# A four-layer transformer block in one launch: another order for the opening, for the modulation sums of one output phase, and for the store of the result

## The chip, the cores and the metric

The kernel runs on one core of one Trainium2 chip. The metric is the device time of one launch in microseconds (us). The time of the kernel before is the median of three runs.

## What is computed

One sequence of 512 tokens by 1024 features (`x`) goes through four layers; from the third on, 256 context tokens come beside it. Each layer first makes six modulation vectors from a condition vector `c`. The first layer, which the change is about, cut to what matters:

```python
cs = jax.nn.silu(c)
ada = cs @ w_ada[i] + b_ada[i]
sh1, sc1, g1, sh2, sc2, g2 = split(ada, 6)
u = x * (1.0 + sc1) + sh1
proj = u @ w_in
qk, v, o, gates = split(proj)
qk = silu(causal_dwconv(qk, conv_w, conv_b))
ig = gates[..., :H]
lf = log_sigmoid(gates[..., H:])
h = chunked_scan(q, k, v, cumsum(lf), ig)
y = (rms_heads(h, norm_g) * sigmoid(o)) @ w_out
x = layer_norm(ALPHA * x + (1.0 + g1) * y, ln_g, ln_b)
```

All of it is float32. What else follows is an FFN with a convolution, a second layer with differential attention, and two more layers with RMS norms, a Fourier mixer, neighbourhood attention and MLPs.

## The kernel before

The activations stand transposed in SBUF: `XT` is 8 tiles (`KT`) of 128 features by 512 tokens. Weights are consumed as a stream of **jobs**: job j is one block of 128 output features, 8 x 128 x 128 weights, 512 KB in `wst`. SyncE loads it into one of two places of `RAW` (`load_raw`, which waits on `lo_done`). A float32 product is made from high and low parts: ScalarE rounds `RAW` to `WH` (`round_hi` and `round_next`, four places), GpSimd subtracts to get `WL` (`lo`), and TensorE multiplies WH by the high part of the activation (`U1h`), WH by the low part (`U1l`), and WL by the high part. So a job is 8 tiles x 3 = 24 matmuls of 128x512 (`stream`). Semaphores `hi_done`, `lo_done`, `pe_job` and `bank_read` count jobs through rounding, low part, matmuls and evacuation. The work is a list of phases (`plan`): "qk" has jobs 0 to 15, "v" 16 to 23, "gate_o" 24 to 31, "res" 32 to 39 (the output projection of layer 0 with residual and LayerNorm statistics), then "up" from job 40 on. Each engine walks the same list with its own code, in the order in which the code is written.

Modulation vectors are **ada sums**: one `tensor_tensor_reduce` of 128x1024 on VectorE for each tile of 128 outputs (`ada_sum`, `ada_job`), with its input tile (512 KB) loaded by SyncE just behind a weight job (`load_ada`, which waits on `ada_done`). `ada_out` adds the bias for four of them into `MOD` and raises `ada_evac`.

The **opening** of the kernel before, engine by engine:

- SyncE loads the condition vector `CB`, then 16 ada tiles into the 8 places of `ADA0`, with the parameters `PRM`, the gate weights `GW`, the whole of `XT` (2 MB, one transfer, behind the 8th ada tile) and the weights of jobs 0 and 1 in between.
- VectorE makes the 16 ada sums, shifts first, scales next (L1650), then `G2` and `B2` for all tiles at once (L1699, L1700), and only then the low parts `U1l` tile by tile (L1688).
- ScalarE rounds `GW` and jobs 0 and 1, then makes `U1h` (L876) and `UF` (L877) of each tile.
- GpSimd makes `GWl` and the low parts of the weights (L556).
- TensorE runs the 24 gate matmuls first (L1421), then the jobs (L1513).
- VectorE then works out the gate rows (`GR`, `GM`, L1706 to L1719, with Exp and Ln on ScalarE, L882 and L883) before it reads the first job's bank with the convolution (`conv`, L1724 and L1726). At the head of the v phase TensorE waits for `gate_rows` and transposes them.

In the **res phase** VectorE's body does, for each job, first `ada_job` and then `epilogue`:

```python
for u in range(4):
    if brings_ada(p, i):
        ada_job(i - p["groups"][0], p["ada"], u)
    epilogue(i, p, u)
```

The epilogue waits for ScalarE's scaled copy `TT` of the bank, adds it to `XT` (L1773), shifts it (L1745) and sums (L1751, L1765). ScalarE squares the shifted tile (L936) before it rounds the next job. After the last job `ln` raises `z_sum`, on which TensorE waits to make the token sums (L1532).

At the **end** SyncE waits for all 8 tiles of `x_final`, stores the 2 MB of `XT` in one transfer (L516) and waits for it.

## Time and profile before

| | |
|---|---|
| median of 3 runs | 2910.82 us (2907.27 to 2913.71) |
| the profiled execution | 2915.03 us |
| its span, first to last instruction | 2913.2 us |
| TensorE busy | 2771.7 us, 95% of the span |
| VectorE / ScalarE / GpSimd busy | 1588.5 / 1047.9 / 1096.3 us |
| mean granted TensorE clock | 0.979 |
| loaded / stored | 322.67 MB / 2.10 MB |

The span is what the rows below are measured in; the profiled execution is 1.8 us longer than its span, and 4.2 us above the median. TensorE is the busiest engine by far, so the time is its busy time and the stretches in which it has nothing to do.

### The profile page before, as it was taken

The page shows a single profiled execution, that of the slowest core. Times are in us where ns is not written, and L with a number is a line of the kernel's source. Part 1 is how long each engine was busy: PE and PEld are TensorE (multiplying, and loading weights), DVE is VectorE, ACT ScalarE, POOL GpSimd, SP SyncE. Part 2 cuts the span into 40 slices and gives each one's busy share as a digit, 9 for nine tenths or more (in the row PEclk, how much of TensorE's full clock was granted, in tenths as well). Part 3 has the DMA queues.
Part 4 walks back from the last instruction along what each step waited for, and adds up shares of the span by engine and source line. Part 5 has one row for each costly group of instructions (what it writes and reads, how often), then busy time and mean ns, then how long its engine had stood idle before and what let it go on. Part 6 is the DMA issues. An engine that isn't in the chain of part 4 may idle for free.

```text
span 2913.2 us, 37874 instructions
## 1 busy us (share of the span) xinstructions
PE 2771.7 (95%) x13936; PEld 2382.2 (82%) x13936; DVE 1588.5 (55%) x2359; ACT 1047.9 (36%) x1695; POOL 1096.3 (38%) x510
## 2 busy tenths in 40 slices
PE   4998899999899899999899999999998999999998
PEld 3885788887776678877899999999997977778887
DVE  6536866966555669987622423755552486332111
ACT  3333353424366453424322322222223348433222
POOL 2440254445422254445422433323335233334442
PEclk9999899999999899999899999999999999999999
DMA  5351345553422135554111122333332122122322
GB/s 213 114 184 49 109 137 190 196 191 117 139 91 62 51 123 188 195 179 148 53 58 59 44 87 87 130 130 130 116 130 73 58 83 77 58 80 94 101 94 87
DMA packets 89816, 328.06 MB, mean 113 GB/s; under 512 B 9940, under 2 KB 10708, under 8 KB 89304
## 3 DMA queue, kind: packets, MB, share of 16 engines
q1 hardware_dynamic: 85392, 312.21, 31.7%
q10 hardware_dynamic: 4296, 14.17, 1.5%
q8 instruction: 78, 1.28, 0.2%
q14 instruction: 50, 0.41, 0.0%
HBM read 322.67 MB, written 2.10 MB: 111 GB/s over the span
## 4 chain that ended last, share of the span: by engine, by line
PE 57%; DVE 2%; POOL 1%; issue 1%; ACT 1%; DVEq 0%; ACTq 0%; POOLq 0%
PE pair L1511 26%; PE pair L1513 18%; PE bank L1513 4%; PE pair L1351 1%; PE pair L1367 1%; PE bank L1384 1%; PE bank L1351 1%; PE pair L1465 1%; PE bank L1441 0%; PE pair L1324 0%; PE bank L1324 0%; PE bank L1304 0%; PE bank L1293 0%; POOL UF L538 0%; DVE UF L2056 0%
## 5 line engine op out<-in xcount | busy, mean ns | idle before, releaser
L556 POOL TENSOR_TENSOR WL<-RAW,WH 128x1024 fp32r<-128x1024 f32 x392 | 986.6, 2518 | 1655.5 <-ACT WH L863 942.3
L863 ACT ACTIVATE WH<-RAW 128x1024 fp32r<-128x1024 f32 x260 | 273.4, 1051 | 328.7 <-PE pair L1511 161.6
L1650 DVE CUSTOM_DVE_ANT_0 ADA<-ADA,CB 128x1024 f32<-128x1024 f32 x128 | 231.9, 1817 | 116.3 <-DMA ADA<-in_ast 104.7
L1783 DVE SCALAR_TENSOR_TENSOR XT<-pair,GATE,XT 128x512 f32 (+1 forms) x96 | 72.0, 750 | 353.7 <-PE pair L1513 179.8
L1511 PE MATMUL pair<-Uh,WH 128*128 128x384 f32 x832 | 215.2, 339 | 3.1 <-issue 1.6
L1511 PE MATMUL pair<-Ul,WH 128*128 128x384 f32 x832 | 211.1, 334 | 0.0
L1511 PE MATMUL pair<-Uh,WL 128*128 128x384 f32 x832 | 211.0, 334 | 0.0
L1513 PE MATMUL bank<-U1h,WH 128*128 128x512 f32 x480 | 187.2, 390 | 0.0
L1513 PE MATMUL bank<-U1h,WL 128*128 128x512 f32 x480 | 186.8, 389 | 0.0
L1513 PE MATMUL bank<-U1l,WH 128*128 128x512 f32 x480 | 186.8, 389 | 0.0
L1513 PE MATMUL pair<-U1h,WH 128*128 128x512 f32 x448 | 175.5, 392 | 2.7 <-POOL WL L556 2.7
L794 ACT ACTIVATE WH<-RAW 128x1024 fp32r<-128x1024 f32 x132 | 139.0, 1054 | 106.3 <-DMA RAW<-in_wst 51.7
L1513 PE MATMUL pair<-Hh,WH 128*128 128x512 f32 x432 | 169.3, 392 | 8.2 <-DVE Hl L648 8.2
L1513 PE MATMUL pair<-U1l,WH 128*128 128x512 f32 x448 | 174.9, 390 | 0.0
L1513 PE MATMUL pair<-U1h,WL 128*128 128x512 f32 x448 | 174.9, 390 | 0.0
L1513 PE MATMUL pair<-Hl,WH 128*128 128x512 f32 x432 | 168.2, 389 | 0.0
L1513 PE MATMUL pair<-Hh,WL 128*128 128x512 f32 x432 | 168.1, 389 | 0.0
L1511 PEld LDWEIGHTS pair<-Uh,WH 128*128 128x128 f32 x832 | 150.1, 188 | 7.3 <-issue 5.3
L1839 DVE SCALAR_TENSOR_TENSOR TT<-pair,TT 128x512 f32<-128x512 f32 x64 | 44.3, 692 | 196.2 <-ACT TT L986 103.7
L1511 PEld LDWEIGHTS pair<-Ul,WH 128*128 128x128 f32 x832 | 150.2, 188 | 0.0
L1511 PEld LDWEIGHTS pair<-Uh,WL 128*128 128x128 f32 x832 | 150.2, 188 | 0.0
L1511 PE MATMUL pair<-Hh,WL 128*128 128x384 f32 x512 | 129.9, 334 | 0.0
(416 smaller groups left out, 6139.1 us busy)
## 6 DMA issues: line engine op xcount, KB each, us to landing
RAW<-in_wst SPq DMA_DIRECT2D x392, 512.0 KB, 3.5
ADA<-in_ast SPq DMA_DIRECT2D x192, 512.0 KB, 4.3
NB<-in_nbias ACTq DMA_DIRECT2D x8, 768.0 KB, 4.5
XT<-in_xt SPq DMA_DIRECT2D x1, 2048.0 KB, 15.4
STRIP<-in_strip ACTq DMA_DIRECT2D x8, 256.0 KB, 2.7
CB<-in_cb ACTq DMA_DIRECT2D x4, 512.0 KB, 4.0
out_xt<-XT SPq DMA_DIRECT2D x1, 2048.0 KB, 6.2
VN<-VN ACTq DMA_DIRECT2D x4, 384.0 KB, 4.5
```

What stands on the lines that cost most here:

```text
L556: pool.tensor_tensor(WL[:, s4], RAW[:, s2], WH[:, s4].bitcast(F32), ALU.subtract)\
L794: act.activation(WH[:, u], RAW[:, u % 2], ACT.Copy).then_inc(S("hi_done"), 1)
L863: act.activation(WH[:, c % 4], RAW[:, c % 2], ACT.Copy).then_inc(S("hi_done"), 1)
L1351: mm = pe.matmul(BANK[b][:], x[:, k, tok], flat(w[:, i, 4 * kk:4 * kk + 4]), start=k == 0 and m == 0, stop=k == KT - 1 and m == 2)
L1367: mm = pe.transpose(BANK[2 + c][:, s * P:(s + 1) * P], ZP[:, i % 3, c, s * P:(s + 1) * P], IDENT[:])
L1384: mm = pe.matmul(BANK[4][64 * c:64 * c + 64, b * P:(b + 1) * P], VN[:, tile, (2 * t + c) * NHD:(2 * t + c + 1) * NHD], PTN[:, i % 2, c, s ...
L1465: pe.matmul(halves(p, u)[0], w[:, u, k], xh[:, k, 0:w0], start=k == 0 and w is WH, stop=False)
L1511: mm = pe.matmul(dst, w[:, u, k], x[:, k, c:c + HALF_TC], start=st and m == 0, stop=en and m == 2)
L1513: mm = pe.matmul(bank_of(p, u)[:], w[:, u, k], x[:, k, 0:T], start=st and m == 0, stop=en and m == 2)
L1650: dve.tensor_tensor_reduce(tile, tile, cb[:, 0], 1.0, 0.0, ALU.mult, ALU.add, AD[:, u, 0:1])\
L1783: ins = dve.scalar_tensor_tensor(out=flat(XT[:, ds(jl, 1)]), in0=bank[:], scalar=gate_of(jl), in1=flat(XT[:, ds(jl, 1)]), op0=ALU.mult, op ...
L1839: ins = dve.scalar_tensor_tensor(out=TT[:, u % 2, 0:T], in0=bank[:], scalar=0.0, in1=TT[:, u % 2, 0:T], op0=ALU.max, op1=ALU.mult)
```

## The change

- **Loads of the opening** go by tile k: the shift and the scale ada tiles of k, the 256 KB of x tile k, and for k < 4 the weights of job k. Jobs 2 and 3 land in the two places of `ADA`, which are free then, so jobs 0 to 3 all have a place of their own (`RAW0`).
- **VectorE** makes the two sums of tile k, `B2` and `G2` of that tile alone, the low part `U1l` of tile k-1, and one low part of weights (jobs 0, 1, the gates, jobs 2, 3), which were GpSimd's. ScalarE follows tile by tile. GpSimd starts with job 4.
- **TensorE** interleaves: as tile k comes it does that tile for each job already begun; job 0 begins with tile 0, job 1 with 1, the gates with 2, job 2 with 3, job 3 with 4. The qk loop then has 12 jobs left.
- **Gate rows** (VectorE, ScalarE) move to the head of the v phase; their transposes and the copy to `COLS` to the head of gate_o.
- **res phase**: `ada_job` stands behind the epilogue of its job instead of ahead of it.
- **Store** of the result: one transfer of 256 KB for each tile as it is final.

```diff
+        RAW0 = [RAW[:, 0], RAW[:, 1]] + [ADA[:, u].rearrange("p (k n) -> p k n", k=KT) for u in range(2)]
...
-            for j in range(16):
-
-                at_least(sp, S("ada_done"), j - 7)
-                sp.dma_start(ADA0[:, j % 8], a["ast"][j]).then_inc(S(f"ada_begin{j % 8}"), 16)
-                if j == 1:
-                    sp.dma_start(PRM[:], a["prm"]).then_inc(S("prm_land"), 16)
-                if j == 3:
+
+            for k in range(KT):
+                for n, j in ((2 * k, k), (2 * k + 1, KT + k)):
+                    at_least(sp, S("ada_done"), n - 7)
+                    sp.dma_start(ADA0[:, n % 8], a["ast"][j]).then_inc(S(f"ada_begin{n % 8}"), 16)
+                    if n == 1:
+                        sp.dma_start(PRM[:], a["prm"]).then_inc(S("prm_land"), 16)
+                sp.dma_start(XT[:, k], a["xt"][:, k]).then_inc(S(f"ada_begin{(2 * k + 1) % 8}"), 16)
+                if k < 4:
+                    sp.dma_start(RAW0[k], a["wst"][k]).then_inc(S(f"raw_land{k % 2}" if k < 2 else f"strip_land{k % 2}"), 16)
+                if k == 1:
                     sp.dma_start(GW[:], a["gw"]).then_inc(S("gw_land"), 16)
-                if j == 7:
-                    sp.dma_start(XT[:], a["xt"]).then_inc(S("x_land"), 16)
-                if j in (10, 12):
-                    load_raw(j // 2 - 5, j // 2 - 5)
+            for u in range(2):
+                sp.sem_inc(S(f"raw_land{u}"), 16)
...
-                        if not (p["j0"] == 0 and is_first(i) and u < 2):
+                        if not (p["j0"] == 0 and is_first(i)):
                             load_raw(i * 4 + (p["j0"] + u), u % 2)
...
-            sp.wait_ge(S("x_final"), KT)
-            sp.dma_start(out, XT[:]).then_inc(S("out_land"), 16)
-            sp.wait_ge(S("out_land"), 16)
+            for t in range(KT):
+                sp.wait_ge(S("x_final"), t + 1)
+                sp.dma_start(out[:, t], XT[:, t]).then_inc(S("out_land"), 16)
+            sp.wait_ge(S("out_land"), 16 * KT)
...
-                for u in range(3):
+                for u in range(3 if p["j0"] else 0):
...
-                lo(p["j0"] + 3, 3, 1)
+                if p["j0"]:
+                    lo(p["j0"] + 3, 3, 1)
...
+                    if c == u + 3 and i == 0:
+                        j = 6 if u == 1 else njobs
...
-            for j in range(2):
-                round_hi(j, j)
-
-
-            act.wait_ge(S("x_land"), 16)
-            act.wait_ge(S("g2_done"), 1)
+            def opening_hi(j):
+
+                if j < 2:
+                    act.wait_ge(S(f"raw_land{j}"), 16)
+                else:
+                    act.wait_ge(S(f"strip_land{j % 2}"), 16)
+                act.activation(WH[:, j], RAW0[j], ACT.Copy).then_inc(S("hi_done"), 1)
+
             for t in range(KT):
+                act.wait_ge(S(f"ada_begin{(2 * t + 1) % 8}"), 32 * (t // 4 + 1))
+                act.wait_ge(S("g2_done"), t + 1)
                 act.activation(U1h[:, t], XT[:, t], ACT.Identity, bias=B2[:, t, 0:1], scale=G2[:, t, 0:1]).then_inc(S("u_hi"), 1)
                 act.activation(UF[:, t, 0:T], XT[:, t], ACT.Identity, bias=B2[:, t, 0:1], scale=G2[:, t, 0:1])\
                     .then_inc(S("uf_done"), 1)
-            round_hi(2, 2)
-
-            act.wait_ge(S("gate_abs"), 1)
-            steps.link(act.activation(GR[0:4, 2], GR[0:4, 1], ACT.Exp))
-            act.activation(GR[0:4, 3], GR[0:4, 2], ACT.Ln, bias=1.0).then_inc(S("gate_ln"), 1)
+                if t < 4:
+                    opening_hi(t)
+                if t == 1:
+                    act.wait_ge(S("gw_land"), 16)
+                    act.activation(GWh[:], GW[:], ACT.Copy).then_inc(S("gate_hi"), 1)
+            round_hi(4, 0)
+            round_hi(5, 1)
+
+            def gate_rows_act():
...
+                    gate_rows_act()
...
+            def opening():
+
+                def gates(k):
+                    if k == 0:
+                        pe.wait_ge(S("gate_lo"), 1)
+                    for m, (w, x) in enumerate(((GWh, U1h), (GWh, U1l), (GWl, U1h))):
+                        mm = pe.matmul(BANK[2][:], w[:, k], x[:, k, 0:T], start=k == 0 and m == 0, stop=k == KT - 1 and m == 2)
+                    if k == KT - 1:
+                        mm.then_inc(S("gates_pe"), 1)
+
+                def job(u, k):
+                    if k == 0:
+                        pe.wait_ge(S("lo_done"), u + 1)
+                    for m, (w, x) in enumerate(((WH, U1h), (WH, U1l), (WL, U1h))):
+                        mm = pe.matmul(bank_of(phases[0], u)[:], w[:, u, k], x[:, k], start=k == 0 and m == 0,
+                                       stop=k == KT - 1 and m == 2)
+                    if k == KT - 1:
+                        mm.then_inc(S("pe_job"), 1)
+
+
+                for k in range(KT):
+                    pe.wait_ge(S("u_ready"), k + 1)
+                    for u, k0 in ((0, 0), (1, 1), (None, 2), (2, 3), (3, 4)):
+                        if k >= k0:
+                            for tile in range(0 if k == k0 else k, k + 1):
+                                if u is None:
+                                    gates(tile)
+                                else:
+                                    job(u, tile)
+
+            opening()
...
                 if first(p, "v", 0):
                     pe.wait_ge(S("const_land"), 16 * 4)
-
+                if first(p, "gate_o", 0):
                     pe.wait_ge(S("gate_rows"), 1)
...
-                if first(p, "res", 1):
+                if p["j0"] == 0:
+                    rounds(pe, p["n"] // 4 - 1, lambda i, p=p: stream(i + 1, p))
+                elif first(p, "res", 1):
...
-            for g in range(4):
-                for u in range(4):
-                    j = 4 * g + u
-                    dve.wait_ge(S(f"ada_begin{j % 8}"), 16 * (j // 8 + 1))
-                    ada_sum(g, 0, u, ADA0[:, j % 8])
-                ada_out(g, 0)
-            dve.wait_ge(S("ada_evac"), 4)
-            link(dve.tensor_scalar(G2[:, :, 0:1], mod(0, 1), 1.0, None, ALU.add))
-            dve.tensor_copy(B2[:, :, 0:1], mod(0, 0)).then_inc(S("g2_done"), 1)
-            u_lo()
...
+            def opening_lo(t):
+                dve.wait_ge(S("uf_done"), t + 1)
+                dve.tensor_tensor(U1l[:, t], UF[:, t, 0:T], U1h[:, t].bitcast(F32), ALU.subtract).then_inc(S("u_ready"), 1)
+
+            for k in range(KT):
+                at_least(dve, S("g2_done"), k - 1)
+                for q in range(2):
+                    n = 2 * k + q
+                    dve.wait_ge(S(f"ada_begin{n % 8}"), (16 + 16 * q) * (n // 8 + 1))
+                    dve.tensor_tensor_reduce(ADA0[:, n % 8], ADA0[:, n % 8], CB[:, 0], 1.0, 0.0, ALU.mult, ALU.add,
+                                             AD[:, n % 4, 0:1]).then_inc(S("ada_done"), 1)
+                dve.wait_ge(S("ada_done"), 2 * k + 2)
+                q = 2 * (k % 2)
+                dve.tensor_tensor(B2[:, k, 0:1], AD[:, q, 0:1], prm("bada", 2 * k), ALU.add)
+                dve.scalar_tensor_tensor(out=G2[:, k, 0:1], in0=AD[:, q + 1, 0:1], scalar=1.0, in1=prm("bada", 2 * (KT + k)),
+                                         op0=ALU.add, op1=ALU.add).then_inc(S("g2_done"), 1)
+                if k >= 1:
+                    opening_lo(k - 1)
+                if k in (0, 1, 3, 4):
+                    j = (0, 1, 1, 2, 3)[k]
+                    dve.wait_ge(S("hi_done"), j + 1)
+                    dve.tensor_tensor(WL[:, j], RAW0[j], WH[:, j].bitcast(F32), ALU.subtract).then_inc(S("lo_done"), 1)
+                if k == 2:
+                    dve.wait_ge(S("gate_hi"), 1)
+                    dve.tensor_tensor(GWl[:], GW[:], GWh[:].bitcast(F32), ALU.subtract).then_inc(S("gate_lo"), 1)
+            dve.wait_ge(S("g2_done"), KT)
+            dve.sem_inc(S("ada_evac"), 4)
+            opening_lo(KT - 1)
+
+            def gate_rows_dve():
+
+                dve.wait_ge(S("gates_pe"), 1)
...
                 if first(p, "v", 0):
+                    gate_rows_dve()
+                if first(p, "gate_o", 0):
...
                     for u in range(4):
-                        if brings_ada(p, i):
+
+                        if brings_ada(p, i) and not first(p, "res", 0):
                             ada_job(i - p["groups"][0], p["ada"], u)
                         epilogue(i, p, u)
+                        if brings_ada(p, i) and first(p, "res", 0):
+                            ada_job(i - p["groups"][0], p["ada"], u)
                     if brings_ada(p, i):
                         ada_out(i - p["groups"][0], p["ada"])
```

TensorE at the very start, before (`pair` and `bank` are PSUM banks, `GWh` and `GWl` the gate weights' parts):

```order
L1421 MATMUL pair<-U1h,GWh 128x512
L1421 MATMUL pair<-U1l,GWh 128x512
L1421 MATMUL pair<-U1h,GWl 128x512
L1421 MATMUL pair<-U1h,GWh 128x512
L1421 MATMUL pair<-U1l,GWh 128x512
```

and now, from the start through tile 1 into tile 2:

```order
L1447 MATMUL pair<-U1h,WH 128x512 [waits lo_done,u_ready]
L1447 MATMUL pair<-U1l,WH 128x512
L1447 MATMUL pair<-U1h,WL 128x512
L1447 MATMUL pair<-U1h,WH 128x512 [waits u_ready]
L1447 MATMUL pair<-U1l,WH 128x512
L1447 MATMUL pair<-U1h,WL 128x512
L1447 MATMUL pair<-U1h,WH 128x512 [waits lo_done]
...
L1447 MATMUL pair<-U1h,WH 128x512 [waits u_ready]
...
L1439 MATMUL pair<-U1h,GWh 128x512 [waits gate_lo]
```

The gates were 24 matmuls ahead of any job; now jobs 0 and 1 begin before them, and the steps for tiles 0 to 7 hold 3, 9, 15, 21, 27, 15, 15 and 15 matmuls.

VectorE in the opening, before (the `ISA` rows are the sums and the reading of their accumulator):

```order
L1650 ISA ADA_65,AD<-ADA_65,CB 128x1024
L1650 ISA AD 128x1
L1662 TENSOR_TENSOR MOD<-AD,PRM 128x4
...
L1699 TENSOR_SCALAR G_81<-MOD 128x8
L1700 COPY B_82<-MOD 128x8
L1688 TENSOR_TENSOR U1l<-UF,U1h 128x512 x8
```

and now, tile 1 of the eight:

```order
L1740 ISA ADA_65,AD<-ADA_65,CB 128x1024
L1740 ISA AD 128x1
L1740 ISA ADA_65,AD<-ADA_65,CB 128x1024
L1740 ISA AD 128x1
L1744 TENSOR_TENSOR B_82<-AD,PRM 128x1
L1745 SCALAR_TENSOR_TENSOR G_81<-AD,PRM 128x1
L1733 TENSOR_TENSOR U1l<-UF,U1h 128x512
L1752 TENSOR_TENSOR WL<-RAW,WH 128x1024
```

The low parts of x stood behind all 16 sums; now each stands behind the sums of the next tile, with a low part of weights (L1752) between.

VectorE at the end of the res phase, before (last job):

```order
L1650 ISA ADA,AD<-ADA,CB 128x1024
L1650 ISA AD 128x1
L1773 SCALAR_TENSOR_TENSOR XT<-XT,TT 128x512
L1745 SCALAR_TENSOR_TENSOR XT<-bank,XT 128x512
L1751 TENSOR_TENSOR ZS<-bank,XT 128x512
L1662 TENSOR_TENSOR MOD<-AD,PRM 128x4
```

and now:

```order
L1831 SCALAR_TENSOR_TENSOR XT<-XT,TT 128x512
L1803 SCALAR_TENSOR_TENSOR XT<-bank,XT 128x512
L1809 TENSOR_TENSOR ZS<-bank,XT 128x512
L1693 ISA ADA,AD<-ADA,CB 128x1024
L1693 ISA AD 128x1
L1705 TENSOR_TENSOR MOD<-AD,PRM 128x4
```

The last ada sum stood ahead of the last residual; now it stands between the last sum of x and the point behind `MOD` where `z_sum` is raised.

## Rows read from the trace of the kernel before

**Rows 1.** Windows: stretch, us, busy of each engine, granted clock, DMA share, GB/s

```profile
0.00:41.40 41.40, 0.00 (x0) 0.03 (x1) 26.85 (x39) 7.90 (x9) 7.23 (x7) 1.00 0.86 347
...
350.00:360.00 10.00, 7.60 (x28) 5.87 (x28) 5.84 (x14) 2.45 (x5) 0.00 (x0) 0.67 0.01 2
```

**Rows 2.** Timeline of VectorE, opening: start us, us, engine, line, operation [idle before]

```profile
8.00 1.22 DVE L1650 CUSTOM_DVE_ANT_0 ADA<-ADA,CB 128x1024 f32<-128x1024 f32 x1 [8.00 <-DMA PRM<-in_prm]
...
9.15 1.22 DVE L1650 CUSTOM_DVE_ANT_0 ADA<-ADA,CB 128x1024 f32<-128x1024 f32 x1
...
22.84 1.23 DVE L1650 CUSTOM_DVE_ANT_0 ADA<-ADA,CB 128x1024 f32<-128x1024 f32 x1 [2.94 <-DMA ADA<-in_ast]
...
27.85 3.31 DVE L1650 CUSTOM_DVE_ANT_0 ADA<-ADA,CB 128x1024 f32<-128x1024 f32 x1 [1.30 <-DMA ADA<-in_ast]
...
38.74 0.17 DVE L1700 COPY B<-MOD 128x8 f32<-128x8 f32 x1
```

**Rows 3.** Timeline of ScalarE and VectorE, first tile of x

```profile
39.01 0.81 ACT L876 ACTIVATE U1h<-XT,B,G 128x512 fp32r<-128x512 f32 x1 [7.65 <-DVE B L1700]
39.73 0.80 ACT L877 ACTIVATE UF<-XT,B,G 128x512 f32<-128x512 f32 x1
...
40.56 0.69 DVE L1688 TENSOR_TENSOR U1l<-UF,U1h 128x512 fp32r<-128x512 f32 x1 [1.65 <-ACT UF L877]
```

**Rows 4.** Timeline of TensorE, first gate matmuls, then the boundary of jobs 3 and 4

```profile
41.97 0.63 PE L1421 MATMUL pair<-U1l,GWh 128*128 128x512 f32 x1
...
42.39 0.63 PE L1421 MATMUL pair<-U1h,GWl 128*128 128x512 f32 x1
...
45.57 0.60 PE L1421 MATMUL pair<-U1h,GWh 128*128 128x512 f32 x1
...
73.54 0.39 PE L1513 MATMUL bank<-U1h,WL 128*128 128x512 f32 x1
73.77 0.39 PE L1513 MATMUL pair<-U1h,WH 128*128 128x512 f32 x1
```

**Rows 5.** Timeline of VectorE and GpSimd, gate rows, first convolution, job 4's low part

```profile
52.19 0.74 DVE L1706 TENSOR_SCALAR GR<-pair,PRM 4x512 f32<-4x512 f32 x1 [1.06 <-PE pair L1421]
...
63.83 0.09 DVE L1719 MEMSET VX<- 128x32 f32 x1
63.95 0.81 DVE L1724 TENSOR_SCALAR TT<-pair,PRM 128x512 f32<-128x512 f32 x1
64.80 2.32 DVE L1726 SCALAR_TENSOR_TENSOR TT<-pair,PRM,TT 128x511 f32<-128x511 f32 x3
...
68.81 2.41 POOL L556 TENSOR_TENSOR WL<-RAW,WH 128x1024 fp32r<-128x1024 f32 x1 [7.55 <-ACT WH L794]
```

**Rows 6.** Timeline of ScalarE, job 19's rounding at the head of the v phase

```profile
143.73 1.06 ACT L794 ACTIVATE WH<-RAW 128x1024 fp32r<-128x1024 f32 x1
```

**Rows 7.** Timeline of three engines and SyncE's queue, end of the res phase

```profile
339.84 0.39 PE L1513 MATMUL bank<-OH,WL 128*128 128x512 f32 x1
...
340.05 0.43 SPq L477 DMA_DIRECT2D ADA<-in_ast  x1
...
340.67 0.68 DVE L1773 SCALAR_TENSOR_TENSOR XT<-XT,TT 128x512 f32<-128x512 f32 x1
...
344.51 2.68 DVE L1650 CUSTOM_DVE_ANT_0 ADA<-ADA,CB 128x1024 f32<-128x1024 f32 x1 [0.98 <-DMA ADA<-in_ast]
...
347.12 0.68 DVE L1773 SCALAR_TENSOR_TENSOR XT<-XT,TT 128x512 f32<-128x512 f32 x1
...
349.29 0.16 DVE L1662 TENSOR_TENSOR MOD<-AD,PRM 128x4 f32<-128x4 f32 x1
```

**Rows 8.** The page's DMA issues: count, KB each, us from issue to landing

```profile
ADA<-in_ast SPq DMA_DIRECT2D x192, 512.0 KB, 4.3
...
STRIP<-in_strip ACTq DMA_DIRECT2D x8, 256.0 KB, 2.7
...
out_xt<-XT SPq DMA_DIRECT2D x1, 2048.0 KB, 6.2
```

More of the change, by code:

```diff
@@ L878, in _ @@
                     .then_inc(S("uf_done"), 1)
[L879 to L883 removed]
+                if t < 4:
[6 more added lines that the diff above has]
+            def gate_rows_act():
+                act.wait_ge(S("gate_abs"), 1)
+                steps.link(act.activation(GR[0:4, 2], GR[0:4, 1], ACT.Exp))
+                act.activation(GR[0:4, 3], GR[0:4, 2], ACT.Ln, bias=1.0).then_inc(S("gate_ln"), 1)
             def ln_act(p, idx):
@@ L1415, in _ @@
         def _(pe):
-            pe.wait_ge(S("gate_lo"), 1)
-            for k in range(KT):
-                pe.wait_ge(S("u_ready"), k + 1)
-                for m, (w, x) in enumerate(((GWh, U1h), (GWh, U1l), (GWl, U1h))):
-                    mm = pe.matmul(BANK[2][:], w[:, k], x[:, k, 0:T], start=k == 0 and m == 0, stop=k == KT - 1 and m == 2)
-            mm.then_inc(S("gates_pe"), 1)
+            def opening():
[24 more added lines that the diff above has]
+            opening()
             def v_turn(i, p, u):
@@ L1683, in rms_gains @@
                 link(dve.tensor_copy(B2[:, :, 0:n], mod(layer, vec, 0, n)))
-            def u_lo():
-                for t in range(KT):
-                    dve.wait_ge(S("uf_done"), t + 1)
-                    dve.tensor_tensor(U1l[:, t], UF[:, t, 0:T], U1h[:, t].bitcast(F32), ALU.subtract).then_inc(S("u_ready"), 1)
             dve.wait_ge(S("prm_land"), 16)
             dve.wait_ge(S("cb_ready"), 1)
-            for g in range(4):
-                for u in range(4):
-                    j = 4 * g + u
-                    dve.wait_ge(S(f"ada_begin{j % 8}"), 16 * (j // 8 + 1))
-                    ada_sum(g, 0, u, ADA0[:, j % 8])
-                ada_out(g, 0)
```

35 lines of the change are left out of this document (15 added, 20 removed).

## The prediction

> **What bounds the kernel.** The page comes first: TensorE is busy 95% of the span, so whatever shortens the time shortens a stretch in which TensorE has nothing to do. The windows show the first such stretch: from 0 to 41.4 us TensorE runs no matmul, while VectorE is busy 26.85 us [rows 1]. The timeline of VectorE there says what the start waits for: sixteen sums one after the other, the first at 8.00 us, `B2` for all tiles at 38.74 us, and only then ScalarE's first tile at 39.01 us and the first low part at 40.56 us [rows 2, 3]. The second stretch is the end of the res phase: the last matmul of job 39 starts at 339.84 us, yet VectorE adds that job's product only at 347.12 us and reaches the point where `z_sum` is raised after 349.29 us [rows 7]. The third is the store: 6.2 us behind the last tile, with nothing beside it [rows 8]. The change touches all three.
>
> **Part 1, the opening.** I rebuild it from durations and take the start of job 4 as the mark, since from there TensorE runs on without a gap. Before, that is 73.77 us [rows 4].
>
> *Loads.* The ninth sum waited for its tile until 22.84 us and the twelfth until 27.85 us [rows 2]. Between them lie two ada tiles, two places further in the queue another one and the weights of job 0, 4 x 0.524 = 2.10 MB in 5.01 us, so 419 GB/s; ahead of the ninth stood 8.35 MB, which puts the start of the flow at 22.84 - 19.9 = 2.9 us. The new opening has 14.1 MB to load. The x tile of k = 0, 1, ... 7 then lands at about 8.5, 12.9, 18.6, 23, 27, 30.5, 33.6 and 36.7 us.
>
> *VectorE.* A sum takes 1.22 us and the next starts 1.15 us behind it [rows 2]. For a tile I take two sums and their drain, 2.4 us, the two 128x1 operations 0.2 us, then a low part of x of 0.65 us [rows 3] and a weight low part of 1.15 us (an estimate: twice the elements of the row of 0.69 us, less a start). ScalarE behind `G2` needs 0.7 + 0.7 us for `U1h` and `UF` [rows 3] and 1.06 us for the rounding of the weights [rows 6]. Tile 0: sums from 8.0, `G2` at 10.7, ScalarE through the weights at 13.3, weight low part to 14.5. Tile 1: `G2` at 17.1, low part of tile 0 at 17.8, weights rounded at 19.7, their low part to 20.9. From tile 2 on ScalarE is early and VectorE runs through: low parts of tiles 1 to 6 at 24.3, 28.7, 33.1, 37.5, 40.7 and 44.0, the last at 45.7 us. Each tile's sums start later than its loads land, by 1.5 us at tile 1 and about 6 us at tile 7, so VectorE sets the pace, not the loads. GpSimd does nothing here, which removes the stretched sums of 3.31 us [rows 2].
>
> *TensorE.* Steps of 3, 9, 15, 21, 27, 15, 15 and 15 matmuls become possible at 17.8, 24.3, 28.7, 33.1, 37.5, 40.7, 44.0 and 45.7 us. In rows at the slow level one starts 0.42 us behind the last, at the fast level 0.23 us [rows 4]; before, that changed 4.2 us after the first one, with short gaps in between. From the step at 33.1 us on the work is without gaps: 93 x 0.227 = 21.1 us, ending at 54.2 us if the 15 before are fast, and at 28.7 + 6.4 + 21.1 = 56.2 us if all of them are slow. I take 55.2. So TensorE's queue of work, not the last tile, sets the end: a few us on VectorE late in the opening cost nothing, one on the path to the fourth step costs itself.
>
> By the Trainium skill (TensorE: Matmul & The Clock Gate, "What's actually happening") an array that was idle before begins at half its clock and rises only after sustained activity; that speaks against work fed in pieces with idle between, and by it the slow end, 56.2 us, would stand in the sum, 1 us more. The slow rows at 41.97 us and the fast ones at 73.54 us agree with it.
>
> *Job 4.* It needs a place of `WH` and bank 0, both free when job 0 ends. Job 0 now ends with the others, 12 matmuls or 2.7 us before the end of the opening, instead of 16 us before it. Behind it come 0.1 + 1.05 us of rounding and 2.4 us on GpSimd [rows 5], 3.6 us plus semaphores, and beside them the convolution, 0.81 + 2.32 us [rows 5]. So job 4 starts about 1.1 us late, at 56.3 us. Jobs 5 to 7 follow each 5.44 us, and GpSimd (2.4 us) and the convolutions (3.1 us) keep ahead. **Gain 73.8 - 56.3 = 17.5 us**, bounds 13 (VectorE 4 us later at the fourth step) and 18.6.
>
> **Part 2, gate rows at the head of v.** They took VectorE from 52.19 to 63.92 us, 11.7 us [rows 5], beside matmuls. They will again: the v phase starts at S, the last convolution ends at S + 3.4, ScalarE comes free from Exp and Ln at about S + 8.3 and then rounds job 19, which it did 4.5 us behind S before (143.73 us [rows 6]). With GpSimd's 2.4 us that job is ready at S + 12, and TensorE wants it at S + 17. VectorE is free at S + 15; the first value tile waits in its bank, and TensorE needs it read only for the third. Cost 0; what hides it is three jobs' matmuls, and if that cover were gone it would cost up to the 11.7 us. The transposes only move. The order of loads in SyncE's queue has the ada loads wait a few us more, with weights for more than a job ahead.
>
> **Part 3, res phase.** Before, a residual every 6.45 us (340.67 to 347.12 [rows 7]) against a job every 5.44 us: each `ada_job` waits for a load (0.98 us), which SyncE sends behind a weight load, which waits for GpSimd, for ScalarE's rounding, for its square, and so for the residual two jobs earlier; and the sum itself takes 2.68 us. With the sum behind the epilogue the same circle spans three jobs, about 12 us or 4 us each, below 5.44, so it no longer sets the pace. VectorE's own work for a job is then 2.9 us of epilogue and 2.7 us of sum if GpSimd runs beside it, 5.6 us, a slip of 0.2 a job or about 1 us in all. The last product is copied by 341.0 us; three operations to 343.1; the last sum 1.2 us and `MOD` 0.2; `z_sum` at 344.7 us, with the slip 345.5. Before, 349.45 us. **Gain 4.0 us**, bounds 4.8 (no slip) and 2.0: even if the last ada tile lands as late as before, at 344.5 us, a sum of 2.68 us and `MOD` end at 347.4. TensorE is idle through this stretch in either order, at a granted clock of 0.67 behind it [rows 1], so all of it counts.
>
> The sum beside GpSimd is where a rule helps: by the Trainium skill (SBUF: State Buffer, "SBUF: two separate sides") an operation with two SBUF inputs on VectorE and one on GpSimd hold a shared pair of ports in turn, for whole instructions. The row of 3.31 us against 1.22 agrees. By it the last sum, with GpSimd idle, is the short one.
>
> **Part 4, the store.** Seven tiles leave while the last ones are computed, a job apart; the last is 256 KB. The nearest row is another transfer of 256 KB, 2.7 us, against 6.2 us for the whole [rows 8]. **Gain 3.5 us**, bounds 3 and 4 (a store is not a load, so half a us either way).
>
> By the fit in the Trainium skill (DMA: Bandwidth & Descriptors, "Anatomy of one DMA") a transfer costs about 2.0 us and its bytes at 436 GB/s, 6.8 and 2.6 us here, so the estimate from that page would be 4.2 us; the rows decide.
>
> **Sum.** 17.5 + 4.0 + 3.5 = 25.0 us: the profiled execution would go from 2915.0 to 2890.0 us. It stands 4.2 us above the median, so the median goes from 2910.8 to about **2886 us**. A measurement of this kernel can tell 0.2%, 5.8 us, from no change.
>
> **Rivals.**
> - *The opening's path on VectorE and ScalarE is longer than I rebuilt it.* The hand-overs at tiles 0 and 1 (ScalarE after `G2`, VectorE after ScalarE) are the only two I found; were there one of 2 us at each of tiles 2 and 3 as well, and 1.15 us too short a weight low part by half for four of them, the fourth step would come 6 us later and job 4 with it: 2892 us. For it: 0.69 us rows are of half the size. Against: ScalarE's work for a tile, 2.5 us, is below VectorE's 4.4.
> - *The gate rows become a wait in v.* VectorE's and ScalarE's 11.7 us come out on TensorE: 2898 us. For it: the chain crosses two engines four times. Against: a 5 us margin at job 19.
> - *TensorE stays at its slow level*, on the side of slower. The steps come with gaps of 5, 0.6 and 1 us at first; if it took all of them slow, 117 matmuls from 24.3 us at 0.42 to 0.43 would end at about 75 us and job 4 start at 76, 19.5 us later than in the forecast, 2905.5 us. Each further job at that level adds 24 x 0.2 = 4.8 us; from the third on the kernel is slower than before by over 0.2%: 2920 us. For it: the window of 350 to 360 us, busy 7.6 of 10, has a granted clock of 0.67 [rows 1]. Against: 0.6 us and 1 us are short gaps, and from 33.1 us on there are none.
> - *The res order does nothing more than its lower bound, and the store likewise*: 2888 us, inside the forecast.
>
> **Chances.** The forecast 0.77 (2879 to 2891), the longer path 0.11, gate rows 0.07, slow level 0.03; 0.02 for no change at all by some mixture. The range of 8 in 10 runs from 2878 (every upper bound, and a median 4 us lucky) to 2897. Faster by over 0.2%: 0.95; within 0.2%: 0.02; slower: 0.03.
>
> **What would show it.** In the changed profile: the first matmul near 18 us and the last of the opening near 55; the first matmul of job 4 near 56; sums of 1.2 us only; low parts of x 4.4 us apart, then 3.2; no wait of TensorE in v; residuals in res every 5.4 to 5.6 us; about 4 us less from the last job of res to the first matmul of the up phase; and eight stores, the last landing under 3 us. A fourth step later than 36 us, a wait for `lo_done` at jobs 19 to 22, or a residual of job 39 more than 3 us behind its last matmul would prove a step wrong.

## The result, and the profile of the changed kernel

| | before | changed |
|---|---|---|
| median of six runs, us | 2913.35 | 2894.53 |
| lowest to highest | 2907.27 to 2915.76 | 2886.27 to 2897.92 |
| profiled execution (span) | 2915.03 (2913.2) | 2896.41 (2894.6) |

The ratio is 0.9929, 95% interval 0.9916 to 0.9941: about 20.7 us faster (the medians stand 18.8 us apart). The forecast was 2886 us, range 2878 to 2897, and 25.0 us in the profiled execution, which shows 18.6. Direction and range held. The size was too large: 2894.5 us lies outside the 2879 to 2891 us to which the forecast gave its chance of 0.77, between the times of two of its rivals.

Both kernels run 13,936 matmuls, from job 4 on the same ones in the same order, but for the transposes of the gate rows, which moved from the head of v to the head of gate_o. Counted back from the last one, a matmul's start before minus its start after is the gain up to there. This ledger of the profiled pair is what the rest explains:

| up to | before, us | gain, us | predicted |
|---|---|---|---|
| first matmul of job 4 | 73.77 | 18.2 | 17.5 |
| head of the res phase | 300.10 | 17.4 | 17.5 |
| last matmul of job 39, res phase | 339.84 | 17.9 | 17.5 |
| token sums behind `z_sum` | 349.38 | 18.7 | 21.5 |
| in the second layer | 1405.06 | 12.9 | 21.5 |
| end of TensorE's work | 2889.95 | 14.5 | 21.5 |
| store landed | end | 18.6 | 25.0 |

The window over the opening, in the columns of [rows 1]:

```profile
0.00:41.40 41.40, 17.89 (x64) 13.27 (x65) 28.24 (x54) 17.68 (x21) 0.21 (x4) 1.00 0.95 373
```

Where TensorE ran no matmul it now has 64 and is busy 17.89 us, while VectorE carries more work than before in the same 41.4 us (28.24 us against 26.85) and GpSimd, with its low parts gone, next to none. The loads take 0.95 of the DMA engines.

VectorE's timeline of the changed opening answers to [rows 2, 3] (`WL` and `RAW` of L1752 are the weight low part, `U1l` of L1733 the low part of x):

```profile
8.02 1.22 DVE L1740 CUSTOM_DVE_ANT_0 ADA<-ADA,CB 128x1024 f32<-128x1024 f32 x1 [8.02 <-DMA PRM<-in_prm]
...
13.66 1.23 DVE L1752 TENSOR_TENSOR WL<-RAW,WH 128x1024 fp32r<-128x1024 f32 x1 [2.60 <-ACT WH L878]
...
17.35 0.69 DVE L1733 TENSOR_TENSOR U1l<-UF,U1h 128x512 fp32r<-128x512 f32 x1
...
20.03 1.22 DVE L1752 TENSOR_TENSOR WL<-RAW,WH 128x1024 fp32r<-128x1024 f32 x1 [1.99 <-ACT WH L878]
...
32.30 0.69 DVE L1733 TENSOR_TENSOR U1l<-UF,U1h 128x512 fp32r<-128x512 f32 x1
...
44.63 0.69 DVE L1733 TENSOR_TENSOR U1l<-UF,U1h 128x512 fp32r<-128x512 f32 x1 [1.05 <-ACT UF L884]
```

Sums are 1.22 us, the first low part ends at 18.0 us and the last at 45.3; the rebuild had 17.8 and 45.7. The two hand-overs between ScalarE and VectorE, 2.60 and 1.99 us, are the two that were foreseen. TensorE, against [rows 4]:

```profile
18.09 0.80 PE L1447 MATMUL pair<-U1h,WH 128*128 128x512 f32 x1 [18.09 <-DVE U1l L1733]
...
27.19 0.63 PE L1447 MATMUL pair<-U1h,WH 128*128 128x512 f32 x1
27.61 0.63 PE L1447 MATMUL pair<-U1l,WH 128*128 128x512 f32 x1
...
28.75 0.50 PE L1447 MATMUL pair<-U1h,WH 128*128 128x512 f32 x1
...
29.32 0.39 PE L1447 MATMUL pair<-U1h,WL 128*128 128x512 f32 x1
29.55 0.40 PE L1447 MATMUL pair<-U1h,WH 128*128 128x512 f32 x1
...
33.04 0.50 PE L1447 MATMUL pair<-U1h,WH 128*128 128x512 f32 x1 [0.60 <-DVE U1l L1733]
...
54.07 0.39 PE L1447 MATMUL bank<-U1h,WL 128*128 128x512 f32 x1
55.55 0.47 PE L1554 MATMUL pair<-U1h,WH 128*128 128x512 f32 x1 [1.09 <-POOL WL L561]
```

From 28.75 us on one matmul starts 0.23 us behind the last (29.32, 29.55), before that 0.42 (27.19, 27.61). The two distances are read here as TensorE's **level**, the lower or the higher of its two clocks (1.2 and 2.4 GHz); the profile's granted clock reads 1.00 over this whole stretch and does not show the step. The last wait of the opening is the 0.60 us ahead of the fourth step, at 33.04. The opening ends at 54.5 (forecast 55.2), and job 4 starts 1.09 us behind it, waiting for GpSimd's low part, at 55.55 (forecast 56.3).

The end of the res phase on VectorE, against [rows 7] (the ada sum is L1693, the residual add L1831):

```profile
317.61 1.23 DVE L1693 CUSTOM_DVE_ANT_0 ADA<-ADA,CB 128x1024 f32<-128x1024 f32 x1
...
318.76 2.87 DVE L1831 SCALAR_TENSOR_TENSOR XT<-XT,TT 128x512 f32<-128x512 f32 x1
...
325.00 2.82 DVE L1831 SCALAR_TENSOR_TENSOR XT<-XT,TT 128x512 f32<-128x512 f32 x1
...
329.31 1.22 DVE L1693 CUSTOM_DVE_ANT_0 ADA<-ADA,CB 128x1024 f32<-128x1024 f32 x1
...
330.58 0.17 DVE L1705 TENSOR_TENSOR MOD<-AD,PRM 128x4 f32<-128x4 f32 x1
```

and GpSimd there:

```profile
317.81 3.29 POOL L561 TENSOR_TENSOR WL<-RAW,WH 128x1024 fp32r<-128x1024 f32 x1 [2.96 <-ACT WH L797]
```

The sum no longer shows 2.68 us, but the add behind it shows 2.82 to 2.87 in place of 0.68, and residuals come 6.24 us apart, not 5.4 to 5.6. TensorE's wait behind job 39 hardly shrinks. The page's line of the store, against [rows 8]:

```profile
out_xt<-XT SPq DMA_DIRECT2D x8, 256.0 KB, 2.1
```

### The profile page after: what moved, and what is told of

It is laid out like the page before. It is cut to its first block, busy times and chain, and to the rows that moved or that the text cites. A ratio compares the mean times of both kernels' runs of the same rounds, so it can differ in the third digit from the quotient of the medians.

```text
span 2894.6 us, 37909 instructions
## 1 busy us (share of the span) xinstructions
PE 2776.9 (96%) x13936; PEld 2387.2 (82%) x13936; DVE 1594.2 (55%) x2374; ACT 1047.4 (36%) x1694; POOL 1090.7 (38%) x505
## 4 chain that ended last, share of the span: by engine, by line
PE 57%; DVE 2%; POOL 2%; issue 1%; ACT 1%; DVEq 0%; ACTq 0%; POOLq 0%
PE pair L1552 26%; PE pair L1554 18%; PE bank L1554 4%; PE pair L1367 1%; PE pair L1383 1%; PE bank L1400 1%; PE bank L1367 1%; POOL UF L543 1%; PE bank L1482 0%; POOL UF L547 0%; PE pair L1340 0%; PE bank L1340 0%; PE bank L1320 0%; PE pair L1506 0%; PE bank L1309 0%
## 5 line engine op out<-in xcount | busy, mean ns | idle before, releaser
L1693 DVE CUSTOM_DVE_ANT_0 ADA<-ADA,CB 128x1024 f32<-128x1024 f32 x112 | 201.7, 1801 | 102.5 <-DMA ADA<-in_ast 99.7
L1554 PE MATMUL bank<-U1h,WH 128*128 128x512 f32 x464 | 181.0, 390 | 0.0
L1554 PE MATMUL bank<-U1h,WL 128*128 128x512 f32 x464 | 180.6, 389 | 0.0
L1554 PE MATMUL bank<-U1l,WH 128*128 128x512 f32 x464 | 180.6, 389 | 0.0
L1554 PE MATMUL pair<-U1h,WH 128*128 128x512 f32 x432 | 169.1, 392 | 3.9 <-POOL WL L561 3.9
L1554 PE MATMUL pair<-U1h,WL 128*128 128x512 f32 x432 | 168.8, 391 | 0.0
L1554 PE MATMUL pair<-U1l,WH 128*128 128x512 f32 x432 | 168.7, 390 | 0.0
L1552 PE MATMUL pair<-Hh,WH 128*128 128x384 f32 x512 | 129.9, 334 | 0.0
```

Source lines behind the costliest of these rows:

```text
L1552: mm = pe.matmul(dst, w[:, u, k], x[:, k, c:c + HALF_TC], start=st and m == 0, stop=en and m == 2)
L1554: mm = pe.matmul(bank_of(p, u)[:], w[:, u, k], x[:, k, 0:T], start=st and m == 0, stop=en and m == 2)
L1693: dve.tensor_tensor_reduce(tile, tile, cb[:, 0], 1.0, 0.0, ALU.mult, ALU.add, AD[:, u, 0:1])\
```

## The experiments

The opening and the store gave about what was forecast, the res phase 0.8 us instead of 4.0, and behind it 4.2 us of gain went away where neither kernel differs. So two questions stood: whether the opening's gain has the causes that the forecast gave it, and what took the rest. For the res phase the theory was the ports that VectorE and GpSimd share, passed on from one operation to the next; for the fall behind it, TensorE's level after gaps, which would differ from one execution to the next, against a wait that the change itself brings.

Gains are against the kernel before, in the same ledger. "Later than the change" compares the start of job 4 with 55.55 us. Part of such a difference is there before any edit acts: the first loads land up to 0.9 us apart in different executions. VectorE's low part of job 0's weights starts at 13.66 us in the changed kernel, at 13.97 in the kernel with the jobs in turn, 14.09 with the gate rows early, 13.99 with the late and 14.34 with the early work.

### Once more the same kernel

> The changed kernel once more, for a second profile. In the first one the gain at matched matmuls was 17.4 us at job 4, 18.7 us at the token sums of the first LayerNorm, and then fell to 12.7 us by 1388 us, where no instruction differs. Theory A (TensorE's clock comes back at a different moment behind each gap, by chance): the small losses stand at other places or are absent, the gain at 1388 us differs by over 1 us. Theory B (the change shifts something that costs later): the same losses at the same places, 12.7 us again within 0.5 us.

2897.38 us, span 2895.6. The gain was 18.2 us at job 4, 18.1 at the token sums, 11.8 at 1405.06 and 13.5 at the end: from the token sums to 1405.06 it falls by 6.3 us, against 5.8 in the first profile, and at the same places. Neither expectation is met in full. The gain at 1405.06 differs by 1.1 us, which is theory A's mark, but half of that was there at the token sums; the places are those of theory B. What it may be is taken up with the late work below.

### The store alone

```diff
-            sp.wait_ge(S("x_final"), KT)
-            sp.dma_start(out, XT[:]).then_inc(S("out_land"), 16)
+            for t in range(KT):
+                sp.wait_ge(S("x_final"), t + 1)
+                sp.dma_start(out[:, t], XT[:, t]).then_inc(S("out_land"), 16)
```

> The kernel before with the result stored tile by tile and nothing else. From the changed profile: the last store lands 2.1 us behind its issue against 6.2 us, so 4.1 us faster, ratio 0.9986. By the page's fit 4.2 us, by the row of the 256 KB load 3.5 us. A rival: the store waits on something else behind the last write and gains under 2 us.

2910.91 us (11 runs) against 2915.26, ratio 0.9987 [0.9978, 0.9996]. The page's line shows 2.1 us in place of 6.2, the 4.1 us of the ledger. The medians differ by 4.4 us and the ratio by 3.8; its interval, 1.2 to 6.4 us, shows a gain but could not tell 4.1 from 3.5.

### The jobs of the opening one after the other

```diff
-                    for u, k0 in ((0, 0), (1, 1), (None, 2), (2, 3), (3, 4)):
...
+                    gates(k)
+                for u in range(4):
+                    for k in range(KT):
+                        job(u, k)
```

> The changed kernel with TensorE's opening in the old order: the gate matmuls tile by tile as low parts of x come, then jobs 0 to 3 one after the other; loads, VectorE and ScalarE as changed. If the interleaving carries the gain as I rebuilt it, the last gate matmul stands at about 45.7 us, 96 matmuls follow to 67.5 us, and job 4 starts at about 67.5 us instead of 55.6 us: 12 us slower than the changed kernel, and only 6 us of the opening's 18 us are left. Rival: the tile-by-tile sums carry it and TensorE's order matters little, under 4 us slower.

2905.68 us, ratio 0.9979 [0.9967, 0.9990]. TensorE is idle between gate matmuls and makes the last of them in slow rows; a row of its timeline:

```profile
46.71 0.63 PE L1439 MATMUL pair<-U1h,GWl 128*128 128x512 f32 x1
```

Job 4 starts at 69.83 us, with a gain of 3.9 us in place of 18.2; the expectation was 67.5. So **14.3 us of the opening's gain (14.0 without the later loads) come from work that TensorE has in its queue while tiles arrive**; loads, sums and low parts tile by tile alone are worth the other 3.9.

### The gate rows where they were

`gate_rows_dve` and `gate_rows_act` are called again at the end of the opening, ahead of the first convolution.

> The changed kernel with the gate rows back at the end of the opening, ahead of the first convolution. With jobs 0 to 3 ending together there is no cover there any more: VectorE is busy with them from about 52.3 to 64 us, bank 0 is read by 67 us instead of 55 us, and job 4 starts 11 to 12 us later, at 67 us. A rival, that they are hidden there as in the kernel before, gives no difference.

2908.29 us, ratio 0.9984 [0.9974, 0.9994]. The kernel's waits of TensorE name the place:

```profile
PE pair L1555 <- DVE TT L1787: 12.1, 1, 12.1
```

Job 4 starts at 66.99 us, 11.4 later than the change (0.4 of it later loads), and the rows behind that wait are slow ones, which costs 2.6 us more by 135 us. Before the change these 11.7 us were free, because TensorE still had jobs 0 to 3 to do; once they end together, the bank of the first job is wanted at once. Moving the gate rows was a condition of the rest.

### Extra work on VectorE, at the last and at the third tile

```diff
+                if k in (7,):          # (2,) in the second kernel
+                    for e in range(3):
+                        cond = CB[:, 0].rearrange("p (a n) -> p a n", a=2)
+                        dve.tensor_tensor(SQ[:, 2 * e:2 * e + 2], cond, cond, ALU.mult)
```

> The changed kernel with three more VectorE operations of 128x1024 (3.5 us, results unused) in the step of tile 7. If TensorE's queue of matmuls sets the end of the opening from the fourth step on, the low parts of the last two tiles come 3.5 us later and job 4 starts at 55.6 us all the same, within 0.5 us. If the last tile sets it, job 4 starts 3.5 us later.

> The same three operations in the step of tile 2, ahead of the low part that allows the second step. Everything on VectorE behind comes 3.5 us later; job 4 starts about 3.5 us later, at 59 us, since the fourth step is on the path. If VectorE were not on the path at all, 55.6 us.

Each carries three products more; in the late one:

```profile
43.24 3.49 DVE L1750 TENSOR_TENSOR SQ<-CB 128x1024 f32<-128x1024 f32 x3
```

Late, job 4 starts at 55.85 us, 0.3 later than the change; at the third tile, at 59.61, 4.1 later. Less the later loads of these two executions (0.3 and 0.7 us) the late work costs nothing and the early work 3.4 of its 3.5 us. The forecast's sentence that the queue of work sets the end held at both places tried. That the border is the fourth step was not tried; it is read from TensorE's rows, whose last wait is the one ahead of that step.

The late kernel, run once, gave a second result: 2885.86 us, 10.5 us less than the changed kernel's profile, with work added. Behind the opening its program is the same. Up to the token sums it is 1.1 us behind the changed kernel; at 1405.06 it is 8.7 ahead, at the end 10.5. One of the places, TensorE in the changed kernel:

```profile
711.47 1.87 PE L1573 MATMUL pair<-MEAN,ZS 128*128 128x1 f32 x8 [0.75 <-DVEq L2033]
713.20 1.84 PE L1573 MATMUL pair<-MEAN,SQ 128*128 128x1 f32 x8
714.91 2.05 PE L1602 MATMUL pair<-ZS,MEAN 128*128 128x512 f32 x2
```

and in the kernel with the late work:

```profile
710.25 1.05 PE L1573 MATMUL pair<-MEAN,ZS 128*128 128x1 f32 x8 [0.75 <-DVEq L2037]
711.17 1.03 PE L1573 MATMUL pair<-MEAN,SQ 128*128 128x1 f32 x8
712.06 1.31 PE L1602 MATMUL pair<-ZS,MEAN 128*128 128x512 f32 x2
```

Windows of 6 us that begin 1.47 us ahead of these rows, first of the changed kernel:

```profile
710.00:716.00 6.00, 5.25 (x25) 4.55 (x24) 2.46 (x9) 1.10 (x3) 0.62 (x1) 0.60 0.50 175
```

and of the one with late work:

```profile
708.78:714.78 6.00, 5.25 (x32) 4.24 (x32) 3.88 (x12) 1.10 (x3) 0.62 (x1) 0.84 0.49 175
```

The same instructions after the same wait of 0.75 us: TensorE is busy 5.25 us in both, at a granted clock of 0.60 in one and 0.84 in the other, so sixteen small products take 3.44 us or 1.81. TensorE's busy time over the span is 2776.9 us in the changed kernel, 2766.1 in the late one, 2771.7 before.

From the token sums to the last matmul, first before, then in the changed kernel (length, TensorE's busy time, matmuls):

```profile
349.38:2889.95 2540.57, 2467.58 (x12643) 0.98 0.33 109
330.67:2875.48 2544.81, 2473.82 (x12642) 0.98 0.33 109
```

TensorE is busy 6.2 us longer with the same matmuls, and idle 2.0 us less. **So the gain that goes away behind the res phase is TensorE's level after short gaps, not work or waits of the change.** It is not a price of the change either: among the eleven other kernels profiled, all but one with the changed opening and all with the same code behind the token sums but for the store or one moved sum, the gain changes over this stretch by anything from -4.7 us (the early work) to +7.4 us (the late work). Which gaps are paid dear was alike in two profiles of the same kernel; whether kernel or execution decides it was not found, since the changed kernel's own executions reach from 2886.3 to 2897.9 us, as far apart as these two.

### Low parts of the opening on GpSimd

The four weight low parts and `GWl` go back from VectorE to GpSimd; all else as changed.

> The changed kernel with the low parts of the gate weights and of jobs 0 to 3 on GpSimd again, the rest as changed. Theory Q (only the path to the fourth step counts): VectorE is spared 5 x 1.15 us and its waits for ScalarE's rounding, but its sums, each with two SBUF inputs, wait for GpSimd's 2.4 us operations, so about 1.3 to 2.2 us are paid back at each of five places; job 4 starts within 2 us of 55.6 us. Theory R (GpSimd's low parts are what held the opening back, so that moving them was needed for the gain): job 4 starts over 5 us later.

2895.87 us, ratio 0.9933 [0.9918, 0.9947]; job 4 at 59.40 us, 3.9 later than the change, between the two expectations (within 2 us, over 5 us), so that neither theory is confirmed. VectorE has less to do, but two sums and, more often, its smallest operation wait:

```profile
14.31 2.96 DVE L1748 CUSTOM_DVE_ANT_0 ADA<-ADA,CB 128x1024 f32<-128x1024 f32 x1 [0.89 <-DMA XT<-in_xt]
...
23.65 2.17 DVE L1752 TENSOR_TENSOR B<-AD,PRM 128x1 f32<-128x1 f32 x1
...
28.82 2.20 DVE L1752 TENSOR_TENSOR B<-AD,PRM 128x1 f32<-128x1 f32 x1
```

and GpSimd beside the last of them:

```profile
28.53 2.47 POOL L570 TENSOR_TENSOR WL<-ADA,WH 128x1024 fp32r<-128x1024 f32 x1 [2.72 <-ACT WH L886]
```

A 128x1 operation of 0.16 us takes 2.2 when it starts behind GpSimd's, and ends with it, at 31.0. Since the first tiles are the path, that costs more than the 1.22 us of a low part on VectorE. The total is not distinguishable from the change (levels again: behind the token sums it lost 0.9 us, the change 4.2).

### ScalarE rounds the weights ahead of the tile of x

`opening_hi(t)` moves in front of ScalarE's wait for `G2`, and the rounding of `GW` with it.

> The changed kernel with ScalarE's rounding of the weights ahead of the activations of each tile, so that VectorE's low part finds it done; in the changed profile VectorE waited for it 2.60 and 1.99 us in the steps of tiles 0 and 1. If the hand-over is the cause, both waits go, and then the loads, which land 1.5 to 6 us ahead now, set the pace at tiles 2 to 4: the fourth step becomes possible near 29.6 us instead of 33.0 us, and job 4 starts at about 53 us instead of 55.6 us. If the loads were the limit already, nothing changes.

2889.37 us, ratio 0.9923 [0.9909, 0.9938]; job 4 at 55.70 us, not at the 53 expected. VectorE's waits for rounded weights shrank from 2.60 and 1.99 us to 0.91 and 0.20, but this execution's first load landed 0.9 us later and the loads of the next tiles set the pace; a wait for `GWh` of 1.2 us came new (`GW` is rounded behind the weights of job 2 there). A miss: what I took from one wait was handed to another.

### The res phase: the old order, the last sum late, the sum inside

Three kernels. `res_order_back` restores the loop body of before in the res phase. `res_last_sum_late` makes the last sum and `MOD` behind the raise of `z_sum`. `res_sum_inside` does that too, and puts every other sum between the shift and the token sums of its job:

```diff
                         .then_inc(S("shifted"), 1)
+                if between:
+                    between()
                 for n, t in ln_slots(idx, jl):
...
                 dve.sem_inc(S("z_sum"), 1)
+                if idx == 0:
+                    ada_job(1, p["ada"], 3)
+                    ada_out(1, p["ada"])
```

> The changed kernel with the ada sum ahead of the epilogue again in the res phase, all else as changed. By the changed profile the new order is worth 1.3 us at the rise of z_sum: expected 1.3 us slower than the changed kernel at the LayerNorm (gain against before 17.4 us there), about 0.9943 of before if the changed kernel is 0.9938. By my prediction's step it would be 4 us slower. The residuals stand 6.5 us apart again.

> The changed kernel with only the last ada sum of the res phase moved behind the rise of z_sum; the other seven stand behind their epilogues. By the row of 1.22 us and the bias of 0.17 us, z_sum rises 1.4 us earlier than in the changed kernel, and residuals still stand 6.25 us apart: a gain of 20.1 us at the token sums instead of 18.7 us. What remains to the 22.7 us of the other variant is what the ports cost in this phase, 2.6 us.

> The changed kernel with each ada sum of the res phase put between the shift of x and the sums of the epilogue, and the last one behind the rise of z_sum. Theory P (the shared ports: sum, GpSimd's low part and the next residual add, each with two SBUF inputs, pass the ports on in turn, 6.25 us a job): the sum is now over before GpSimd starts, the residual add takes 0.7 us instead of 2.8 us, residuals stand 5.44 us apart, and the rise of z_sum comes about 3.0 us behind the last matmul of job 39 instead of 8.3 us: 4.5 to 5 us faster than the changed kernel. Theory L (the circle of loads still sets the pace): residuals stay over 6 us apart and only the last sum's 1.4 us is gained.

| kernel | gain from the last matmul of job 39 to the token sums, us | ratio to before |
|---|---|---|
| old order | -0.4 | 0.9918 [0.9904, 0.9931] |
| changed | 0.8 | 0.9929 [0.9916, 0.9941] |
| last sum late | 2.0 | 0.9919 [0.9905, 0.9933] |
| sum inside | 5.7 | 0.9909 [0.9894, 0.9924] |

VectorE with the sum inside:

```profile
318.58 1.20 DVE L1833 SCALAR_TENSOR_TENSOR XT<-XT,TT 128x512 f32<-128x512 f32 x1 [0.96 <-ACT TT L1011]
...
320.42 1.22 DVE L1693 CUSTOM_DVE_ANT_0 ADA<-ADA,CB 128x1024 f32<-128x1024 f32 x1
...
324.02 1.09 DVE L1833 SCALAR_TENSOR_TENSOR XT<-XT,TT 128x512 f32<-128x512 f32 x1 [1.04 <-ACT TT L1011]
```

and GpSimd:

```profile
316.84 2.39 POOL L561 TENSOR_TENSOR WL<-RAW,WH 128x1024 fp32r<-128x1024 f32 x1 [2.97 <-ACT WH L797]
```

Residuals come 5.44 us apart, TensorE's own pace, and VectorE waits for ScalarE instead of the reverse. GpSimd's low part is 2.39 us again instead of 3.29, and the add 1.1 to 1.2 instead of 2.87. Only the place of a 1.22 us sum among the five operations of a job was moved, and the last one of the phase. The same kernel shows which operations wait. L1825 adds the squares; at the first tile it reads them from SBUF alone, at the next also a sum in PSUM (`pair`):

```profile
300.03 2.85 DVE L1825 TENSOR_TENSOR pair<-SQ 128x512 f32<-128x512 f32 x1
...
306.12 0.70 DVE L1825 TENSOR_TENSOR pair<-pair,SQ 128x512 f32<-128x512 f32 x1
```

GpSimd's low parts started 0.1 us ahead of each:

```profile
299.93 2.39 POOL L561 TENSOR_TENSOR WL<-RAW,WH 128x1024 fp32r<-128x1024 f32 x1 [3.42 <-ACT WH L797]
306.03 2.40 POOL L561 TENSOR_TENSOR WL<-RAW,WH 128x1024 fp32r<-128x1024 f32 x1 [3.71 <-ACT WH L797]
```

The one waited 2.2 us, the other not at all. With the sum inside the gain at the token sums is 22.7 us, 4.0 above the change, or 4.9 counted from job 39 (expected 4.5 to 5); with only the last sum late it is 20.9 (expected 20.1), 0.9 us of which was there already at job 39. In the total, the four kernels of the table can't be told apart, their intervals overlap: the order alone is worth 1.2 us at the token sums and the sum inside 4.9 more, below or near what levels do to a run. The reading rests on the rows.

### Both together

> Both improvements together: ScalarE's weights first, and in the res phase the sum between shift and sums with the last one behind z_sum. They stand far apart and should add: job 4 at about 53 us and a gain at the rise of z_sum of about 25 us against before (22.7 us with the second alone); about 2883 us.

Weights rounded first, and the sum inside: 2884.67 us (4 runs, 2879.37 to 2885.68) against 2915.3, ratio **0.9892** [0.9877, 0.9906], whose interval lies below the change's. Job 4 starts at 54.13 us, the gain at the token sums is 25.2 us. This is the fastest version run. How much of its opening is ScalarE's new order stays open, since the same opening code had job 4 at 55.70 in the kernel above, where the first sum started 0.9 us later. With the first sum at 7.98 us, as good as the changed kernel's 8.02, job 4 came 1.4 us earlier than there; that is one execution of each.

## Why the prediction was right, and where it was not

**Part 1, opening: right.** 18.2 us at job 4 against 17.5. The chain of sums, hand-overs and low parts on VectorE came within 0.4 us at every tile (low parts of x end at 18.0, 24.4, 28.7 and so on to 45.3); the 0.7 us more are TensorE's faster rows, from 28.75 us on and not from 33.1, so the opening ended at 54.5 us and not at 55.2. The forecast took the slow end of 56.2 us to follow from the Trainium skill (TensorE: Matmul & The Clock Gate, "What's actually happening"), where the array's clock rises after sustained activity. The trace agrees with the page and not with that use of it: the fast rows begin behind nine matmuls made one after the other from 24.46 us on, in spite of the waits ahead of them. The three supports of the term were each tested: the queue (14.3 us lost without it), the late tile that costs nothing (0.3 us for 3.5 of work, all of it later loads), the early one that costs itself (4.1 us, of which 0.7 are later loads).

**Part 2, gate rows: right.** They ran from 124.71 to 139.9 us on VectorE beside matmuls, with v from S = 120.95 us. ScalarE rounded job 19 at 130.80 us, S + 9.9 (forecast S + 8.3), its low part was ready at 135.1 and TensorE took it up at 138.7, so 3.6 us of the forecast margin of 5 were left. TensorE's waits for VectorE or ScalarE in v came to 0.6 us, against 0.3 before; its gain was 18.1 us ahead of v and 17.4 at the head of res, so the cost was at most 0.7 us. The counter-test shows what they would cost in the old place, 11.4 us.

**Part 3, res phase: the step that failed.** The sentence was "VectorE's own work for a job is then 2.9 us of epilogue and 2.7 us of sum if GpSimd runs beside it, 5.6 us, a slip of 0.2 a job". It measured 6.24 us, and the term 0.8 us instead of 4.0. I counted one meeting with GpSimd, priced at 2.68 - 1.22 = 1.46 us, as in [rows 7]. The changed order has a full round: GpSimd's operation arrives 0.2 us behind the sum and waits for its end (3.29 instead of 2.39), the residual add stands right behind and waits for all of GpSimd's, 2.87 - 0.69 = 2.18 us. Sum and epilogue without GpSimd are 1.15 + 4 x 0.73 = 4.07 us, and 4.07 + 2.18 = 6.25, the pace of the rows. The forecast had said that a residual over 3 us behind its last matmul would prove a step wrong; it came 325.00 - 321.90 = 3.1 us behind and then waited 2.1 more. The experiment confirms the cause: with two operations between sum and add, both with an input in PSUM, the pace is TensorE's and 4.9 us return, of which the last sum behind `z_sum` is 1.2 to 1.3.

The rule quoted there, from the Trainium skill (SBUF — State Buffer, "SBUF: two separate sides"), that the pair of ports is held for whole instructions, agrees with these rows, and was applied to the sum alone. By it each operation in the queue has to be asked, not only the long one. By the same rule an operation that has one input in PSUM does not ask for the pair; the rows of L1825, 0.70 us beside GpSimd with such an input and 2.85 us without, agree.

**Part 4, store: right in kind, low by 0.6 us.** 4.1 us against 3.5, by the small transfer's 2.1 us where I took a load's 2.7. The estimate from the Trainium skill (DMA: Bandwidth & Descriptors, "Anatomy of one DMA"), 4.2 us, was the nearer, though its fit is of transfers that GpSimd issues and these are SyncE's; its two durations, 6.8 and 2.6 us, are 0.6 and 0.5 above the rows.

**What no term had.** From the token sums to the end the profile gives 4.2 us back (18.7 to 14.5), more than all of it in TensorE's level. The sum of the terms as measured, 18.2 + 0.8 + 4.1 = 23.1 us, less these 4.2 and 0.3 lost between job 4 and job 39 (gate rows or level, not told apart) is the 18.6 of the profile. Of the miss of 6.4 us part 3 is 3.2 and the two losses are 4.5, while parts 1 and 4 gave 1.3 back. No rival came in: the opening's path was not longer, gate rows were no wait, TensorE rose early. Part 3 fell below its own lower bound of 2.0, which had a late ada tile in it but not the ports. That the median stayed within the range owes something to luck: the range had no term for levels, whose share in one execution can be as large as the whole miss.

## What to carry to other kernels

While inputs arrive piece by piece, give TensorE the work of several jobs that each piece makes possible, so that its queue outlasts the last piece; then only the path to the step from which the queue no longer empties counts, and whatever read the old order's results (here the gate rows) has to leave that place too. Where VectorE and GpSimd share a loop, look at the pair of neighbours in VectorE's queue around the moment GpSimd starts: a VectorE operation with two SBUF inputs right behind another one pays for GpSimd's whole instruction, and one that reads PSUM is a good thing to put there. A moved operation is best priced by the pace of the whole round, not by its own duration.

## What was not expected of the hardware

- Executions of one program spread from 2886.3 to 2897.9 us, 0.4%. Two kernels with the same code behind the opening differ as much, and there the difference sits in TensorE's level behind gaps of under 1 to 5 us: 1.6 us at one layer norm, 10.8 us of busy time over the span. That the spread of one program has the same source was not shown: its two profiles were alike. By the Trainium skill (TensorE: Matmul & The Clock Gate, "What's actually happening") the count of slow matmuls at a kernel's start differs between runs of one kernel; no two profiles here show that for one kernel, but the pair of kernels shows it at gaps all along the span. An edit worth 1 to 4 us is read from the ledger of matched matmuls, not from the median.
- A 128x1 operation on VectorE took 2.20 us behind GpSimd, fourteen times its 0.16.
- Stores of 256 KB, issued by SyncE, landed in 2.1 us, loads of the same size, issued by ScalarE, in 2.7. Whether direction or queue makes the difference was not tried.
